# A hybrid decoder step on one core: state-space loads two chunks later in SyncE's order, and another start of the first stage

## The reference, cut to what matters

```python
def mixer_layer(x, past, ...):
    q, k, v, gate_a, qi, ki, wi, u, gate_s, qm, gate_m = project(x, g_norm, w_in)   # rmsnorm(x, g_norm) @ w_in, split
...
    o_s, h_re, h_im = s5_branch(u, h0_re, h0_im, lam_re, lam_im, log_dt, b_re, b_im, c_re, c_im, d_skip, w_glu)
    o_m = mem_attend(qm, mem_k, mem_v)
    mix = jnp.concatenate([o_a * jax.nn.silu(gate_a), o_s * jax.nn.silu(gate_s), o_m * jax.nn.silu(gate_m)], axis=-1)
    y = x + mix @ w_out

def mem_kv(mem, g_mem, w_mem_kv):
    kv = rmsnorm(mem, g_mem) @ w_mem_kv
```

## Time and profile before

| what | value |
|---|---|
| median of three runs | 2072.8 us (2068.49 to 2073.71) |
| the profiled execution's own time | 2071.27 us |
| its span in the trace | 2069.7 us, 31722 instructions |
| TensorE matmul busy | 1858.3 us (90%) |
| VectorE, ScalarE, GpSimd busy | 1096.8 us (53%), 839.5 us (41%), 293.7 us (14%) |
| mean granted clock of TensorE | 0.956 |
| projection matmuls, L644 | 948.4 us busy in 6096 matmuls, 6.4 us idle just before them |
| first stage | from 0 to 112 us |
| projection | from 112 to 1169 us |

### The profile page before, as it was taken

How to read it: one execution, slowest core, us unless ns; L and a number is a source line. 1 busy time by engine, 2 the same in 40 slices (tenths; PEclk the granted TensorE clock), 3 DMA queues, 4 the chain that set the end, 5 groups by cost and what they waited for, 6 DMA issues and landing times. The chain is left out here.

```text
span 2069.7 us, 31722 instructions
## 1 busy us (share of the span) xinstructions
PE 1858.3 (90%) x12951; PEld 1267.6 (61%) x12951; DVE 1096.8 (53%) x2047; ACT 839.5 (41%) x1447; POOL 293.7 (14%) x182
## 2 busy tenths in 40 slices
PE   5979999997999999999999797898888459898997
PEld 3555555554666666666666457555455138787886
DVE  5544045558777866867765025665535762221225
ACT  4454467663344334434343004543336153342431
POOL 3012211111112111211121001220013040000000
PEclk9989999998999999999999899999999669999999
DMA  7522211113232222223211452102027021212124
GB/s 274 168 82 62 79 50 63 42 42 90 67 90 70 82 80 78 68 80 86 80 62 55 170 205 63 31 21 56 1 58 264 29 82 63 63 63 63 63 70 182
DMA packets 186952, 175.92 MB, mean 85 GB/s; under 512 B 27382, under 2 KB 168342, under 8 KB 184054
## 3 DMA queue, kind: packets, MB, share of 16 engines
q1 hardware_dynamic: 166742, 133.18, 20.6%
q10 hardware_dynamic: 14496, 22.95, 3.0%
q0 software_dynamic: 5568, 17.72, 2.5%
HBM read 139.65 MB, written 34.17 MB: 84 GB/s over the span
## 5 line engine op out<-in xcount | busy, mean ns | idle before, releaser
L644 PE MATMUL ps<-h,w 128*128 128x352 f16 (+2 forms) x6096 | 948.4, 316 | 6.4 <-POOL w L917 6.1
L644 PEld LDWEIGHTS ps<-h,w 128*128 128x128 f16 (+1 forms) x6096 | 597.4, 99 | 340.4 <-issue 15.3
L2140 PE MATMUL ps<-w_f,m 128*128 128x256 f16 x3072 | 351.0, 278 | 33.1 <-POOL w_f L2079 16.9
L2140 PEld LDWEIGHTS ps<-w_f,m 128*128 128x128 f16 x3072 | 304.5, 100 | 78.0 <-POOL w_f L2079 17.9
L917 POOL TENSOR_TENSOR w<-wb,w 128x2048 f16<-128x2048 f32 (+1 forms) x45 | 186.6, 4147 | 859.1 <-ACT w L776 859.1
L784 ACT ACTIVATE zst<-ps,unit 128x352 f32<-128x352 f32 (+1 forms) x112 | 63.1, 576 | 327.7 <-PE ps L644 303.6
L1116 DVE MAX8 m<-score 128x8 f32<-128x1024 f32 (+2 forms) x192 | 171.6, 894 | 5.7
L2205 DVE SCALAR_TENSOR_TENSOR y_room<-ps,unit_f,x_f 128x256 f32 (+1 forms) x64 | 31.0, 484 | 266.2 <-PE ps L2140 241.8
L1117 DVE MATCH_REPLACE8 score<-m,score 128x1024 f32<-128x1024 f32 (+2 forms) x192 | 168.1, 876 | 0.0
L1108 DVE SCALAR_TENSOR_TENSOR score<-room,wis,score 128x1024 f32<-128x1024 f32 (+5 forms) x90 | 92.3, 1026 | 79.4 <-ACT room L839 74.3
L758 ACT ACTIVATE absolute<-wb 128x512 bf16<-128x512 f32 (+1 forms) x180 | 112.3, 624 | 35.3 <-DMA wb<-in_w_in_dram 25.0
(11 more groups left out here) (409 smaller groups left out, 1813.2 us busy)
## 6 DMA issues: line engine op xcount, KB each, us to landing
wb<-in_w_in_dram SPq DMA_DIRECT2D x44, 1024.0 KB, 5.2
z_scratch<-zst ACTq DMA_DIRECT2D x32, 528.0 KB, 2.7
score<-in_w_out_dram SPq DMA_DIRECT2D x8, 2048.0 KB, 11.6
y_room<-z_scratch SPq DMA_DIRECT2D x8, 1056.0 KB, 17.5
w_kv<-in_w_mem_kv_dram POOLq DMA_DIRECT2D x16, 512.0 KB, 4.3
x_in<-in_x_prompt_dram SPq DMA_DIRECT2D x8, 1024.0 KB, 4.9
x_f<-in_x_prompt_dram SPq DMA_DIRECT2D x8, 1024.0 KB, 5.3
out_y_p_dram<-y_room SPq DMA_DIRECT2D x8, 1024.0 KB, 3.9
```

What stands on the lines that cost most here:

```text
L644: last = nc.tensor.matmul(ps[0:m, n, 0:w], w16[:, b, pw_, k, 0:m], h16[:, ph, k, t0:t0 + w], start=(k == 0 and i == 0), stop=(k == KT - 1 ...
L2140: last = nc.tensor.matmul(ps[:, bank(b, t), 0:SLAB], m16[:, mp, k, t * P:(t + 1) * P], w16[:, b, wp, k, :], start=(k == 0 and j == 0), sto ...
```

## The change

Part one is in block_a. The rows `x_in` have three buffers instead of two. In SyncE's order the rows of a tile come before the norm weight, and waits begin with tile 3. The bound of the norm weight is taken from `g_norm` laid out as 128 x 16, which ScalarE's queue loads; VectorE reduces 16 columns, TensorE transposes the 128 maxima, VectorE reduces them, and TensorE spreads the one value with a product with ones. `g_norm` itself is no longer scaled; instead each prompt tile's reciprocal is. GpSimd makes its constants first, then issues four loads of `w_kv`, then those of the parameters. `cnat` moves from a buffer of its own into the unused half of `wb`.

Part two is in block_b: load_u stands at x == 3 instead of x == 1, and spread_kernels at x == 5 instead of x == 3. Two semaphores (`last_turned`, `kv_stored_c`) are merged into others, with the waits' values raised to fit.

```diff
-        x_in = sb("x_in", [P, 2, D_MODEL])
-        cnat = sb("cnat", [P, 2, BATCHES, 2, STATE])
+        IN = 3
+        x_in = sb("x_in", [P, IN, D_MODEL])
...
+        cnat = v["wb"][:, 1, 6:6 + 2 * BATCHES, :].rearrange("p (n j) (a s) -> p n j a s", n=2, a=2)
...
@@ block_a, sync
             for t in range(ALL):
-                b, n = t % 2, rows(t)
+                b, n = t % IN, rows(t)
+                if t >= IN:
+                    sp.wait_ge(squares, t - IN + 1)
+                    sp.wait_ge(h_ready, t - IN + 1)
+                sp.dma_start(x_in[0:n, b, :], source(t)).then_inc(x_loaded[b], 16)
                 if t < 2:
                     g = io["g_norm" if t else "g_mem"]
                     sp.dma_start(g_b[:, t, :], g[0].partition_broadcast(P)).then_inc(g_loaded[t], 16)
-                if t >= 2:
-                    sp.wait_ge(squares, t - 1)
-                    sp.wait_ge(h_ready, t - 1)
-                sp.dma_start(x_in[0:n, b, :], source(t)).then_inc(x_loaded[b], 16)
@@ block_a, gpsimd
+            link(nc.gpsimd.memset(ident[:], 0.0))
...
+            nc.gpsimd.memset(v["ones"][:], 1.0).then_inc(consts_ready, 1)
...
+            for k in range(4):
+                load_w_kv(k)
             pool.dma_start(lam_in[:, 0, :], io["lam_re"][0].rearrange("(i a) n -> i (a n)", a=2)).then_inc(params_loaded, 16)
...
-            link(nc.gpsimd.memset(ident[:], 0.0))
...
-            nc.gpsimd.memset(v["ones"][:], 1.0).then_inc(consts_ready, 1)
-            for k in range(KT):
-                if k >= 4:
-                    pool.wait_ge(kv_step, k - 3)
-                pool.dma_start(w_kv[:, k % 4, :], io["w_mem_kv"][0, k * P:(k + 1) * P, :]).then_inc(w_kv_loaded[k % 4], 16)
+            for k in range(4, KT):
+                pool.wait_ge(kv_step, k - 3)
+                load_w_kv(k)
@@ block_a, scalar
+            act.dma_start(g_col[:], io["g_norm"][0].rearrange("(p k) -> p k", k=KT)).then_inc(g_col_loaded, 16)
@@ block_a, vector
+            dve.wait_ge(g_col_loaded, 16)
+            nc.vector.tensor_reduce(g_max[:, 0:1], g_col[:], AX_X, ALU.max)
+            link(nc.vector.tensor_reduce(g_max[:, 1:2], g_col[:], AX_X, ALU.min))
+            link(nc.vector.tensor_scalar(g_max[:, 1:2], g_max[:, 1:2], -1.0, TINY, ALU.mult, ALU.max))
+            nc.vector.tensor_tensor(g_max[:, 0:1], g_max[:, 0:1], g_max[:, 1:2], ALU.max).then_inc(g_reduced, 1)
+            dve.wait_ge(g_spread, 1)
+            nc.vector.tensor_reduce(g_max[0:1, 2:3], ps[0:1, 7, 0:P], AX_X, ALU.max).then_inc(g_reduced, 1)
+            dve.wait_ge(g_spread, 2)
+            link(nc.vector.tensor_scalar(h_unit[:], ps[:, 7, P:P + 1], 1.0 / ROOT_H, None, ALU.mult))
+            link(nc.vector.reciprocal(inv_unit[:], h_unit[:]))
...
-                    if t == 0:
-                        dve.wait_ge(g_loaded[0], 16)
-                        dve.wait_ge(g_loaded[1], 16)
-                        g = g_b[:, 1, :]
-                        nc.vector.tensor_reduce(g_max[:, 0:1], g, AX_X, ALU.max)
-                        link(nc.vector.tensor_reduce(g_max[:, 1:2], g, AX_X, ALU.min))
-                        link(nc.vector.tensor_scalar(g_max[:, 1:2], g_max[:, 1:2], -1.0, TINY, ALU.mult, ALU.max))
-                        link(nc.vector.tensor_tensor(g_max[:, 0:1], g_max[:, 0:1], g_max[:, 1:2], ALU.max))
-                        link(nc.vector.tensor_scalar(h_unit[:], g_max[:, 0:1], 1.0 / ROOT_H, None, ALU.mult))
-                        link(nc.vector.reciprocal(g_max[:, 1:2], h_unit[:]))
-                        link(nc.vector.tensor_scalar(g, g, g_max[:, 1:2], None, ALU.mult))
+                    if t < 2:
+                        dve.wait_ge(g_loaded[t], 16)
+                    if t >= MT:
+                        link(nc.vector.tensor_scalar(stat[0:n, 2, t:t + 1], stat[0:n, 2, t:t + 1], inv_unit[0:n, :], None, ALU.mult))
@@ block_a, tensor
             pe.wait_ge(ident_ready, 1)
+            pe.wait_ge(g_reduced, 1)
+            nc.tensor.transpose(ps[0:1, 7, 0:P], g_max[:, 0:1], ident[:]).then_inc(g_spread, 1)
+            pe.wait_ge(g_reduced, 2)
+            pe.wait_ge(consts_ready, 1)
+            nc.tensor.matmul(ps[:, 7, P:P + 1], v["ones"][0:1, :], g_max[0:1, 2:3], start=True, stop=True).then_inc(g_spread, 1)
@@ block_b, sync
                 t, x = turn(c)
-                if x == 1:
+                if x == 3:
                     load_u(t)
-                if x == 3:
+                if x == 5:
                     spread_kernels(t)
@@ block_b, tensor and vector
-                    last.then_inc(last_turned, 1)
+                    last.then_inc(turned, 1)
...
-                    dve.wait_ge(last_turned, 1)
+                    dve.wait_ge(turned, 2)
@@ block_c
-            sp.wait_ge(kv_stored, 64)
+            sp.wait_ge(kv_stored, 32 + 64)
```

More of the change, by code:

```diff
@@ L205, in block_a @@
         g_b = sb("g_b", [P, 2, D_MODEL])
-        g_max = sb("g_max", [P, 2])
+        g_col = sb("g_col", [P, KT])
+        g_max = sb("g_max", [P, 3])
+        inv_unit = sb("inv_unit", [P, 1])
         memT = sb("memT", [P, KT, N_MEM])
@@ L215, in block_a @@
         st_in = v["wb"][:, 1, 4:6, :]
+        cnat = v["wb"][:, 1, 6:6 + 2 * BATCHES, :].rearrange("p (n j) (a s) -> p n j a s", n=2, a=2)
         dt_in = sb("dt_in", [TILES, 2])
-        x_loaded = [sem(f"x_loaded{b}") for b in range(2)]
+        x_loaded = [sem(f"x_loaded{b}") for b in range(IN)]
+        g_col_loaded, g_reduced, g_spread = sem("g_col_loaded"), sem("g_reduced"), sem("g_spread")
         g_loaded = [sem("g_mem_loaded"), sem("g_norm_loaded")]
@@ L274, in _, with load_w_kv @@
             link = v["pool_chain"].on(pool)
+            link(nc.gpsimd.memset(ident[:], 0.0))
+            nc.gpsimd.affine_select(out=ident[:], in_=ident[:], compare_op=ALU.not_equal, fill=1.0, base=0,
+                                    pattern=[[-1, P]], channel_multiplier=1).then_inc(ident_ready, 1)
+            link(nc.gpsimd.memset(cmin[:], 3e38))
+            link(nc.gpsimd.affine_select(out=cmin[:], in_=cmin[:], compare_op=ALU.is_ge, fill=INVALID, base=0,
+                                         pattern=[[-1, P]], channel_multiplier=1))
+            for k in range(10):
+                link(nc.gpsimd.memset(pw[:, k:k + 1], float(2**k)))
+            nc.gpsimd.memset(v["ones"][:], 1.0).then_inc(consts_ready, 1)
+            def load_w_kv(k):
+                pool.dma_start(w_kv[:, k % 4, :], io["w_mem_kv"][0, k * P:(k + 1) * P, :]).then_inc(w_kv_loaded[k % 4], 16)
+            for k in range(4):
+                load_w_kv(k)
             pool.dma_start(lam_in[:, 0, :], io["lam_re"][0].rearrange("(i a) n -> i (a n)", a=2)).then_inc(params_loaded, 16)
@@ L328, in _ @@
         def _(act):
+            act.dma_start(g_col[:], io["g_norm"][0].rearrange("(p k) -> p k", k=KT)).then_inc(g_col_loaded, 16)
             for t in range(ALL + 1):
                 if t < ALL:
-                    b, n = t % 2, rows(t)
-                    act.wait_ge(x_loaded[b], 16 * (t // 2 + 1))
+                    b, n = t % IN, rows(t)
+                    act.wait_ge(x_loaded[b], 16 * (t // IN + 1))
                     nc.scalar.activation(sq[0:n, :], x_in[0:n, b, :], ACT.Square,
@@ L360, in _ @@
                     link(nc.vector.reciprocal(stat[0:n, 2, t:t + 1], rms[0:n, t:t + 1]))
-                    if t == 0:
-                        dve.wait_ge(g_loaded[0], 16)
-                        dve.wait_ge(g_loaded[1], 16)
-                        g = g_b[:, 1, :]
-                        nc.vector.tensor_reduce(g_max[:, 0:1], g, AX_X, ALU.max)
-                        link(nc.vector.tensor_reduce(g_max[:, 1:2], g, AX_X, ALU.min))
-                        link(nc.vector.tensor_scalar(g_max[:, 1:2], g_max[:, 1:2], -1.0, TINY, ALU.mult, ALU.max))
-                        link(nc.vector.tensor_tensor(g_max[:, 0:1], g_max[:, 0:1], g_max[:, 1:2], ALU.max))
-                        link(nc.vector.tensor_scalar(h_unit[:], g_max[:, 0:1], 1.0 / ROOT_H, None, ALU.mult))
-                        link(nc.vector.reciprocal(g_max[:, 1:2], h_unit[:]))
-                        link(nc.vector.tensor_scalar(g, g, g_max[:, 1:2], None, ALU.mult))
+                    if t < 2:
+                        dve.wait_ge(g_loaded[t], 16)
+                    if t >= MT:
+                        link(nc.vector.tensor_scalar(stat[0:n, 2, t:t + 1], stat[0:n, 2, t:t + 1], inv_unit[0:n, :], None, ALU.mult))
                     if t >= 2:
                         dve.wait_ge(h_transposed, 4 * (t - 1))
-                    nc.vector.scalar_tensor_tensor(out=h_tok[0:n, b, :], in0=x_in[0:n, b, :], scalar=stat[0:n, 2, t:t + 1],
+                    nc.vector.scalar_tensor_tensor(out=h_tok[0:n, b, :], in0=x_in[0:n, t % IN, :], scalar=stat[0:n, 2, t:t + 1],
                                                    in1=g_b[0:n, int(t >= MT), :], op0=ALU.mult, op1=ALU.mult).then_inc(h_ready, 1)
```

3 lines of the change are left out of this document (1 added, 2 removed).

## The result

The changed kernel took 2046.53 us, median of four runs (2044.05 to 2051.07), beside 2072.41 for the kernel before; the ratio is 0.9881 with a 95% interval of 0.9859 to 0.9903, so 20 to 29 us less. It is faster, as forecast, and by more: the forecast was 2053.4 with a range down to 2048.5. The profiled execution is the slowest of the four, 2051.07 us around a span of 2049.5, and its span is 20.2 us shorter than the profiled one of before.

A forecast was written before the change was run, and what follows sets the result against it. TensorE's matmuls fill nine tenths of the span, so only its idle and slow-clock time can be won. 15.2 us in the projection plus 4.2 in the first stage, 19.4 us, took 2072.8 to 2053.4 us, range 2048.5 to 2061.

The forecast's parts named there:

- 15.2 us: Projection, first turn: with chunk 17 loaded before load_u(0), TensorE reaches drive(0) 15.2 us earlier, at 506.5 instead of 521.75.
- cover of 1.4 us: At chunk 17, its split is ready at 507.2 and TensorE comes to it at 508.6, so no wait.
- the second turn's margin: Moved u loads follow chunk 25's load at 648.7; drive(1) wants them at 683.16, 27 us away; they land in 1.7 to 2.5.
- (c): Rival, projection: moving load_u does nothing because chunk 17 is late for another reason; 2068.6 us, chance 0.04.
- (d): Rival, turns 1 to 3: moved u loads come too late for drive, so slower; 2098 us at 40 us landing, chance 0.03.
- the other 3.77 MB at 236 take 16.0 us: First stage: after 1.47 MB at 387 GB/s, SyncE's remaining bytes before the third tile's rows move at 236 GB/s beside GpSimd's queue.
- 4.2: First stage: TensorE starts the third tile at 28.2 instead of 32.39, a gain of 4.2 us.
- estimate by the Trainium skill: First stage: SyncE's queue gets two thirds of the bandwidth, 258 GB/s; third tile's rows at about 21.5, gain 5.6 us.
- My bound on that side, 10.5: First stage's upper bound: if GpSimd's queue took nothing, 5.24 MB at 387 GB/s are seen at 16.6, gain 10.5 us.
- its lower end: Lowest time of the range, 2048.5 us: 15.2 in the projection, 6.5 in the first stage, and 2.6 of spread.
- Half the spread of three runs, 2.6 us: Whole kernel: allowance for differences between runs, 2.6 us, used at both ends of the range.
- (a): Rival, first stage: GpSimd's earlier w_kv loads push the third tile's rows to 27.8, losing the gain; 2058.3 us, chance 0.12.

The follow-up runs named there:

- e2: The kernel before with load_u and spread_kernels two chunks later and nothing else; 2059.39 us, ratio 0.9930.
- e11: The kernel before with only load_u moved, to x == 3, and spread_kernels left at x == 3 behind it; 2057.28 us in one run.
- e7: The changed kernel with twelve selection rounds instead of eight at x == 0 of each turn, as many in all; 2056.85 us.
- e12: The changed kernel with load_u at x == 4 and spread_kernels at x == 6, one chunk later still; 2057.81 us in one run.
- e4: The changed kernel with GpSimd's 15 parameter loads ahead of its first four w_kv loads; 2048.51 us.
- e6: The changed kernel with GpSimd waiting for two squared tiles before its first w_kv load, the parameters held back too; 2045.1 us, ratio 0.9880.
- e1: The changed kernel timed again in five runs, no edit; 2049.65 us, ratio 0.9879.
- e5: The changed kernel with two row buffers instead of three; 2052.03 us.
- e8: The changed kernel with each turn's 24 stores of y issued by SyncE instead of ScalarE; 2041.0 us, ratio 0.9846.

## Why the prediction was right or wrong

**Part two was right, in its mechanism and its size.** 15.2 us were worked out from the earlier trace rows; 15.5 were measured, by itself (e2), with one of its halves (e11) and in the whole. The new wait's cover of 1.4 us was measured as 1.5, and e7 shows what lies behind it. One number was off by 1 us and harmless: from 648.7 and 8.5 us of transfers to 683.16 it is 26 us, not 27. That SyncE's later waits hold nothing back, and that the second turn's margin is wide, is shown by e12, where one chunk more costs only in turn 0. Rivals (c) and (d) did not come.

**Part one had the right mechanism and a term that was too small.** The step that failed is "the other 3.77 MB at 236 take 16.0 us: rows complete at 22.5, seen at about 22.9". They were seen at 19.71. Two numbers in it were off. First, SyncE's queue had the engines alone for longer than 6.5 us: its share was still 87.9% from 6 to 9 us, by the view of the DMA queues of the changed kernel in that stretch:

```profile
q1 hardware_dynamic: 152, 1.11, 87.9%
```

Second, beside `w_kv` it moved 1.97 MB in 7 us, 281 GB/s, and not the 236 of the earlier trace rows. That row was taken beside the parameters, whose small pieces lower the rate of all traffic; e4 shows this, 215 GB/s for SyncE's queue beside them from 12 to 16 us and 288 beside `w_kv`. With the measured rates in the prediction's sum (370 GB/s from 6.5 to 9 us, then 281) the rows are complete at 19.1 and seen at 19.5, so the two account for the 3.2 us by which the rows came early, to within 0.2; the chain behind them was 5.31 us where 5.25 were worked out. 4.2 became 7.4.

The share itself was what the prediction's estimate by the Trainium skill (DMA: Bandwidth & Descriptors, Queues, rings and completion order) gave, two thirds: the changed kernel's row shows 67.0% beside 34.5%. By that estimate's own sum the gain was 5.6, still too little, since it too started from 387 GB/s for the engines and from 6.5 us.

My bound on that side, 10.5 if GpSimd's queue took nothing, held for this change but was itself too low: in e6, where that is so, SyncE's queue moved 427 GB/s and not 387, and the third tile's transposes start 11.3 us earlier than before. What failed with the range was its lower end. It took 6.5 us for the first stage. The traced gains, 7.5 + 15.5 = 23.0 from 2072.8, are 2049.8, inside the range; the four runs' median of 2046.5 lies another 3 us lower, and no trace explains those 3 us. Nine runs have 2048.67. Half the spread of three runs, 2.6 us, was too small an allowance, for the kernel before itself ran from 2068.13 to 2081.49 in later runs. What makes executions of one kernel differ by such amounts was only seen in part. Falls of the clock cost 1.7 us each at two waits of 1.7 us, and come in some executions and not in others. More comes behind the projection, where no edit changes the work: between its end and the end of the span the traces lose up to 2.5 us against the kernel before (e1, e11) or win up to 5.0 (e6). Why they do is open.

**What the prediction left unsaid.** It called the third buffer what lets the request go early ("With three buffers that request no longer waits for anything"). e5 shows that the buffer is worth nothing there: with the bound off the path, the first tile is multiplied at 12.0 us, while the engines still work at the four transfers ahead, and the request finds a full queue either way. It also had `g_col` there at about 3.5 us; it came at 6.11, and the chain behind it took 2.5 us where 3 were given. That cost nothing, since VectorE's first product waits for ScalarE's root until 9.47.

**(a)**, that `w_kv`'s earlier loads give the gain back, was right in its mechanism and not in its size: without them 12.49 us are gained (e6), with them 7.49. That is the largest thing the change left lying in the first stage; in the projection ScalarE's issuing of the stores costs more, 6.7 us and the falls of the clock behind it (e8).

## What to carry to other kernels

A queue that carries prefetches in order should not stand in a wait while a load behind it is due; follow what is next in that engine's program, and move the waiting step to where nothing behind it may go anyway, but no further than its own consumer allows. At a stage's start, first take long work on late data off the path, as the bound of the norm weight here. When the start is then bound by DMA bandwidth, the order of bytes over all queues counts more than buffers or early requests: hold back what is wanted later, even if its engine is idle. A rate read from one mix of traffic is not the rate of another mix.

## What the runs showed of the hardware that was not expected

Small pieces cost the large transfers beside them more than their share of the engines. From 12 to 16 us in e4 they took 23.4% of the engines' time, and SyncE's 8 KB pieces moved 0.86 MB in 74.0% of it; beside the 4 KB pieces of `w_kv` the same queue moved 1.15 MB in 67.8%.

TensorE's clock fell to 1.2 GHz in some executions at waits of 1.7 us and not in others of the same kernel, at 1.7 us a time. At the waits of 0.6 to 1.5 us in the third and fourth turn no trace shows a fall. So a kernel with two such waits differs from itself by up to 3.4 us for that reason alone.
